# Expert pairs on column halves: w1/w3 products of both experts together, norm factor in the SiLU step, a fourth w2 buffer, and an output tail in pieces

## What is computed

```python
def hier_moe(h, w_grp, b_grp, w_exp, b_exp, w1, w3, w2):
    t = h.reshape(-1, D)                       # h = rms_norm(x, norm2_g)
    pg = softmax(t @ w_grp + b_grp)            # 4 groups, top 1
    el = (t @ w_exp + b_exp)[chosen group]     # 8 experts of it, top 2
    ...
    hid = silu(einsum('td,edf->tef', t, w1)) * einsum('td,edf->tef', t, w3)
    hid = hid * combine[..., None]
    out = einsum('tef,efd->td', hid, w2)
# x = x + hier_moe(rms_norm(x, norm2_g), ...), then the final norm
```

## Time and profile before

| what | us |
|---|---|
| median of 3 runs | 1255.3 (1254.24 to 1257.63) |
| the profiled execution | 1259.09 |
| its span (first to last instruction) | 1257.4 |
| TensorE busy in the span | 1195.2 |
| VectorE busy | 707.4 |
| ScalarE busy | 408.1 |
| GpSimd busy | 37.8 |

### The profile page before, as it was taken

The page is one execution under the profiler, slowest core; times in us unless marked ns, Lnnn a source line. Parts: engine busy times, 40 slices in busy tenths (PEclk is TensorE's granted clock), DMA queues, the critical chain, the costliest instruction groups (busy, mean ns, idle before and its releaser), DMA issues.

```text
span 1257.4 us, 19349 instructions
## 1 busy us (share of the span) xinstructions
PE 1195.2 (95%) x7286; PEld 898.5 (71%) x7286; DVE 707.4 (56%) x1006; ACT 408.1 (32%) x462; POOL 37.8 (3%) x53
## 2 busy tenths in 40 slices
PE   7999999999999999999999998999999999999994
PEld 6888888888888888888888888555555444444441
DVE  5777555554666767667875546344554444444445
ACT  4444333334344354443344542111112111111113
POOL 1000000001002022000000000000000000000000
PEclk8999999999999999999999999999999999999998
DMA  8566565655655455555765683999999999999993
GB/s 273 169 192 208 168 193 174 190 177 167 197 164 166 142 167 167 167 167 190 247 178 164 231 306 127 363 405 425 425 425 425 426 425 425 425 424 425 425 424 147
DMA packets 170150, 336.57 MB, mean 268 GB/s; under 512 B 12144, under 2 KB 136192, under 8 KB 153088
## 3 DMA queue, kind: packets, MB, share of 16 engines
q1 hardware_dynamic: 165536, 335.69, 72.5%
q10 hardware_dynamic: 4576, 0.37, 0.3%
HBM read 333.93 MB, written 2.11 MB: 267 GB/s over the span
## 4 chain that ended last, share of the span: by engine, by line
PE 57%; issue 40%; DVE 1%; DMA 1%; ACT 0%; ACTq 0%; POOL 0%; POOLq 0%; DVEq 0%
PE ps L830 19%; PE ps L859 11%; PE ps L832 10%; PE ps L861 5%; PE ps L991 5%; PE ps L992 2%; PE ps L819 1%; DMA param_rows<-in_norm_g_dram 1%; PE ps L960 0%; PE ps L1011 0%; DVE wsplit L1176 0%; PE ps L846 0%; PE ps L848 0%; ACT wsplit L582 0%; PE ps L847 0%
## 5 line engine op out<-in xcount | busy, mean ns | idle before, releaser
L1176 DVE TENSOR_TENSOR wsplit<-wraw,wsplit 128x2048 fp32r<-128x2048 f32 x120 | 277.1, 2309 | 183.2 <-ACT wsplit L582 182.3
L830 PE MATMUL ps<-act_split,wsplit 128*128 128x512 f32 x1024 | 362.0, 398 | 0.0
L582 ACT ACTIVATE wsplit<-wraw 128x2048 fp32r<-128x2048 f32 x120 | 230.0, 1917 | 387.4 <-PE ps L832 203.1
L832 PE MATMUL ps<-act_split,wsplit 128*128 128x256 f32 x1024 | 286.6, 280 | 0.0
L830 PEld LDWEIGHTS ps<-act_split,wsplit 128*128 128x128 f32 x1024 | 192.2, 188 | 47.7 <-issue 1.8
L859 PE MATMUL ps<-wsplit,act_split 128*128 128x512 f32 x608 | 218.3, 403 | 2.1 <-DVE wsplit L1176 2.1
L832 PEld LDWEIGHTS ps<-act_split,wsplit 128*128 128x128 f32 x1024 | 193.2, 189 | 0.2
L861 PE MATMUL ps<-wsplit,act_split 128*128 128x256 f32 x608 | 171.4, 282 | 0.0
L859 PEld LDWEIGHTS ps<-wsplit,act_split 128*128 128x128 f32 x608 | 115.7, 190 | 30.7 <-issue 2.7
L1082 PE MATMUL ps<-w_a,xe 128*64 128x256 f32 x1024 | 115.4, 381 | 14.3 <-DMA w_a<-in_w_dram 12.1
L1647 DVE TENSOR_TENSOR hid<-sg,ps 128x128 f32<-128x128 f32 x32 | 9.2, 287 | 205.8 <-ACT sg L775 205.8
(11 more groups left out here) (287 smaller groups left out, 1149.8 us busy)
## 6 DMA issues: line engine op xcount, KB each, us to landing
w_a<-in_w_dram SPq DMA_DIRECT2D x96, 1024.0 KB, 18.3
w_b<-in_w_dram SPq DMA_DIRECT2D x96, 1024.0 KB, 22.0
wraw<-in_w_in_dram SPq DMA_DIRECT2D x88, 1024.0 KB, 5.1
wraw<-in_w_out_dram SPq DMA_DIRECT2D x16, 1024.0 KB, 5.1
wraw<-in_w_branch_m_dram SPq DMA_DIRECT2D x8, 1024.0 KB, 5.1
wraw<-in_w_branch_a_dram SPq DMA_DIRECT2D x8, 1024.0 KB, 5.1
xin<-in_x_dram SPq DMA_DIRECT2D x2, 1024.0 KB, 6.3
x<-in_x_dram SPq DMA_DIRECT2D x1, 2048.0 KB, 9.4
```

What stands on the lines that cost most here:

```text
L582: act.activation(wsplit[:, q % 2, :, 0], wraw[:, q % RAW], ACT.Copy).then_inc(rounded, 1)
L830: pe.matmul(banks[b], w[:, k, 0, b * P:(b + 1) * P], a, start=first and k == 0, stop=False)
L832: last = pe.matmul(banks[b][:, 0:T], w[:, k, 1, b * P:(b + 1) * P], a[:, 0], start=False, stop=last_half and k == HALF_K - 1)
L1176: dve.tensor_tensor(wsplit[:, q % 2, :, 1], wraw[:, q % RAW], wsplit[:, q % 2, :, 0].bitcast(F32), ALU.subtract).then_inc(split, 1)
```

## The change

1. **Hidden products by pairs.** `hidden` now takes both experts of a pair at once: for each chunk one matmul of 512 columns (w1 and w3 whole) for the first expert on column half 0 and one for the second on column half 1. There are 32 matmuls a pair, which were 64 of 256 columns. One sigmoid, two products, two transposes and one copy follow for both experts together. `xe` is two buffers.
2. **Norm factor.** `xe` is a plain copy of `xg`; the 17th gather group goes. Two small matmuls make a row `rms_row` of all tokens' factors instead, and VectorE's new step in `slots` picks the factor of each slot by it (`slot_rms`). The sigmoid takes it as its scale and the two products take it and `slot_both` (factor times slot weight) as scalars, so that w2's result needs no scaling. `slots` now runs ahead of the sigmoid.
3. **Loads.** w1/w3 buffers are in quarters: DMAs of 0.5 MiB with runs of 4 KB, twice as many. Each quarter of both experts is loaded again when `h_quarters` says that it is done. w2 of expert 0 moves to its own place (`x2hi` goes to where `x2` was, ScalarE's copy to `x2` falls away, and `make_x2` adds x2hi and x2lo to `x2` in two VectorE steps of 128x2048 in front of the first `slots`), and is loaded in front of w1/w3 of expert 1. w2 waits for each half of `rows`.
4. **First pair.** Its `xe_first` has a place of its own: the first expert's is copied by ScalarE, 12 chunks between the last evacuations (L782) and 4 behind the table load; the second's by VectorE.
5. **Scatter.** Groups 0, 1 behind the first quarter, 2, 3 behind the second, 4 to 7 behind the last.
6. **Tail.** `rows` of the last pair is cut after block 2, two groups of scatter lie between; rounding and subtraction of its right half are in two pieces; groups use four banks. The multiply by final_g moves from VectorE to GpSimd, in front of the root.

```diff
-        w2s = [[sb("w2_a0", [P, FC, D], at=AT_GATES + 32 * KB), sb("w2_b0", [P, FC, D], at=AT_WRAW + 32 * KB)],
+        w2s = [[sb("w2_a0", [P, FC, D], at=AT_QK + 16 * KB), sb("w2_b0", [P, FC, D], at=AT_WRAW + 32 * KB)],
...
-            for kh in range(2):
-                load_hidden(0, 0, kh)
+            for kq in range(QUARTERS):
+                load_hidden(0, 0, kq)
+            for h in range(2):
+                load_rows(0, 0, 0, h)
...
-            sp.wait_ge(xg_summed, DC + 1)
-            load_rows(0, lambda b: b, (0,))
...
-                    for b in range(2):
-                        sp.wait_ge(upper_used, i * (2 * chunks) + (2 * chunks - 1 + b))
-                        load_hidden(b, ds(i * 2 + (b + 2), 1), 0)
-                        sp.wait_ge(h_summed, i * (2 * chunks) + (2 * chunks + b))
-                        load_hidden(b, ds(i * 2 + (b + 2), 1), 1)
+                    for kq in range(QUARTERS):
+                        sp.wait_ge(h_quarters, (i - 1) * (QUARTERS * chunks) + (QUARTERS * (chunks - 1) + kq + 2))
+                        for b in range(2):
+                            load_hidden(b, ds(i * 2 + b, 1), kq)
...
+            pool.wait_ge(fing_loaded, 16)
+            for g, (t, n) in enumerate(tail_groups):
+                pool.wait_ge(x2_final, g + 1)
+                cols = slice(n * 512, (n + 1) * 512)
+                pool.tensor_tensor(x2g[:, t, cols], x2[:, t, cols], fin_g[:, cols], ALU.mult).then_inc(x2g_ready, 1)
             root(42, TT, M_HEADS + 3)
...
+            def silu_and_turn(s):
+
+                act.wait_ge(h_quarters, s * QUARTERS + (QUARTERS + 1))
+                act.wait_ge(slots_ready, s + 2)
+                act.wait_ge(hid_ready, s + 1)
+                act.activation(sg[:], ps[:, 0, 0:FC * P], ACT.Sigmoid, scale=slot_rms[:, 0:1]).then_inc(sg_ready, 1)
+                act.wait_ge(hid_turned, s + 2)
+                act.wait_ge(y_summed, s * 4 + 1)
+                act.activation(hidT[:].rearrange("p f n -> p (f n)"), ps[:, 1, 0:FC * P], ACT.Copy).then_inc(hidT_ready, 1)
...
+                for kq in range(QUARTERS):
+                    pe.wait_ge(w13_loaded[kq], i * 64 + 64)
+                    for k in range(QUARTER_K):
+                        for b in range(2):
+                            last = pe.matmul(ps[b * SLOTS:(b + 1) * SLOTS, 0].rearrange("p (w f) -> p w f", w=2),
+                                             operands[b][:, kq * QUARTER_K + k], w13[b][:, kq, :, k],
+                                             start=kq == 0 and k == 0, stop=kq == QUARTERS - 1 and k == QUARTER_K - 1)
+                    last.then_inc(h_quarters, 1)
...
+            def silu(s):
+
+                dve.wait_ge(sg_ready, s + 1)
+                dve.wait_ge(hid_turned, s + 1)
+                dve.wait_ge(slots_ready, s + 2)
+                steps_x.done(dve.scalar_tensor_tensor(hid[:], ps[:, 0, 0:FC * P], slot_rms[:, 0:1], sg[:], ALU.mult, ALU.mult))
+                dve.scalar_tensor_tensor(hid[:], ps[:, 0, FC * P:2 * FC * P], slot_both[:, 0:1], hid[:],
+                                         ALU.mult, ALU.mult).then_inc(hid_ready, 1)
```

More of the change, by code:

```diff
@@ L1060, in _ @@
             parts = [part[:].rearrange("p t (q c) -> p t c q", c=DC) for part in (x2hi, x2lo)]
[L1061 to L1063 removed]
+            for c in range(DC):
+                if c >= 8:
+                    pe.wait_ge((xg_act, xg_dve)[c % 2], (c - 8) // 2 + 1)
                 for t in range(TT):
[L1065 to L1067 removed]
@@ L1102, in rows, with turn_mix @@
-            def rows(load_no, s, slot):
-                pe.wait_ge(hidT_ready, s * 2 + 3)
+            pe.wait_ge(xg_dve, 5)
+            for t in range(TT):
+                last = pe.matmul(ps[:, 1, t * P:(t + 1) * P], ones[:], rms_diag[:, t], start=True, stop=True)
+            last.then_inc(rms_summed, 1)
+            def turn_mix(s):
+                pe.wait_ge(mix_ready, s + 1)
+                pe.wait_ge(slots_ready, s + 1)
+                pe.wait_ge(hidT_ready, s + 1)
+                for t in range(TT):
+                    last = pe.transpose(ps[:, 1, (FC + t) * P:(FC + t + 1) * P], mix[:, t], ident[:])
+                last.then_inc(mix_turned, 1)
@@ L1105, in rows, with turn @@
+            def turn(s):
+                pe.wait_ge(hid_ready, s + 2)
+                pe.wait_ge(hidT_ready, s + 1)
+                pe.wait_ge(slots_ready, s + 2)
+                for f in range(FC):
+                    last = pe.transpose(ps[:, 1, f * P:(f + 1) * P], hid[:, f * P:(f + 1) * P], ident[:])
+                last.then_inc(hid_turned, 1)
+            def rows(load_no, s, slot, ns=range(4)):
+                pe.wait_ge(hidT_ready, s + 2)
                 pe.wait_ge(ys_ready, s * 2 + 1)
-                for n in range(4):
+                for n in ns:
@@ L1148, in experts @@
+                turn(0)
                 rows(0, 0, 0)
[L1150 to L1162 removed]
@@ L1163, in experts, with hidden_and_scatter @@
-                pair(EXPERTS // 2 - 1, EXPERTS // 4 - 1, 1)
-                scatter(EXPERTS // 2 - 1, range(GROUPS_OUT))
+                def hidden_and_scatter(i, half):
+                    hidden(i, i, xe, [[lambda: scatter(i - 1, half, (0, 1))], [lambda: scatter(i - 1, half, (2, 3))],
+                                      [], [lambda: scatter(i - 1, half, (4, 5, 6, 7))]])
+                    turn(i)
+                with pe.Fori(0, N_PAIRS // 2 - 1) as j:
+                    hidden_and_scatter(j * 2 + 1, 0)
+                    rows(j, j * 2 + 1, 1)
+                    hidden_and_scatter(j * 2 + 2, 1)
+                    rows(j + 1, j * 2 + 2, 0)
@@ new lines, in pair @@
+                def pair(i, half):
+                    ys_split(i - 1)
+                    slots(i, half, (i - 1) * GROUPS_OUT + 1)
+                    add(i - 1, (0, 1, 2, 3))
+                    silu(i)
+                    add(i - 1, (4, 5, 6, 7))
+                with steps_x.loop(0, N_PAIRS // 2 - 1, 4) as j:
+                    for n in (1, 2):
+                        i = j * 2 + n
+                        pair(i, n % 2)
+                        copy_tokens(starts_of(i + 1, 0), i + 1)
+                        make_mix(i + 1, 0, i + 1)
```

387 lines of the change are left out of this document (191 added, 196 removed).

## The result

The changed kernel takes **1260.17 us** (median of 19 runs, 1255.44 to 1263.33), the kernel before 1255.42 beside it (1253.92 to 1260.02): ratio 1.0028, interval 1.0019 to 1.0037. That is 3.5 us slower, 2.4 to 4.6 by the interval. The forecast was 1253.0 with a range to 1258.5: the time lies outside it. The profiled run of after is one of its short ones: 1257.89 us, span 1256.2.

What follows compares the result with a forecast made beforehand. The prediction took the stream of expert weights to bound the expert stage. Its terms, -7.5 (start) + 5.7 (rate) + 0.3 (pair) - 0.95 (tail), gave -2.4 us and a forecast of 1253 us, range 1246.5 to 1258.5.

Steps and rivals of the forecast that it cites:

- What bounds the kernel: Expert stage: set by the stream of expert weights at 425 GB/s, 29.6 us a pair; TensorE waits in nearly every pair.
- All 16 pairs run behind the stream: Expert stage: every pair is paced by the weight stream, 29.59 us a pair, read from two issues six pairs apart.
- Part 1: Start of the weight stream: w2 of expert 0 loaded early and experts starting sooner move it from 794.9 to 787.4, gain 7.5 us.
- No pause: Start of the weight stream: after the change, places come free early enough that the stream doesn't stop again.
- Part 2: Rate of the weight stream: w1/w3 transfers cut in two, with 4 KB runs, cost 0.047 us a MiB over 120 MiB, +5.7 us.
- Part 3: Inside a pair: TensorE 27.9 us before, 27.7 after, hidden behind the stream except in the last pair, +0.3 us.
- still covered by 2.3 us: Inside a pair: TensorE's 27.7 us stay 2.3 us under the stream's 30.0, so only the last pair counts.
- Part 4: Tail, from the last w2 product to the end of the root: 19.25 us instead of 20.2, -0.95 us.
- R: Start of the last w2 product, from which the tail's times are counted; 1229.12 in the kernel before.
- the pause stays: Rival, start of the stream: it isn't continuous and the pause of 3.0 us stays, +0.6, 1256 us; 6%.
- TensorE becomes the bound: Rival, expert stage: needs 2.3 us more a pair, hidden steps of 0.50 instead of 0.43; +42 at 0.59; 3%.

Runs made afterwards that it cites:

- e5: e1 with SyncE requesting the w2 of pairs 3 to 10 before their w1/w3 instead of behind: 1257.06 us, ratio 0.9992 to the kernel before.
- e6: e1 with the prefetch undone, w2 of expert 0 requested after the gather again: 1257.68 us, ratio 1.0007 to the kernel before.
- e1: The changed kernel with filler matmuls where TensorE idles between the w1/w3 and w2 products: 1258.62 us, ratio 1.0013 to the kernel before.
- e3: The kernel before with each w1/w3 transfer cut in two along K (0.5 MiB, 4 KB runs), nothing else: 1262.76 us, ratio 1.0038.
- e12: The changed kernel with only the 4 filler matmuls behind scatter group 5: 1261.87 us, ratio 1.0042 to the kernel before.

## Why the prediction was wrong, step by step

- **What bounds the kernel: half right.** "All 16 pairs run behind the stream" rested on issues at 1007.85 and 1185.36, both in the second half. In the timeline of before, pairs 1 to 7 take 27.40 us without a wait for weights, and only from pair 8 on 29.6; the 15 waits of the earlier trace rows are about two in each of the late pairs, not one in nearly every pair. The places are full when the experts begin, and TensorE lives on that. Two issues in the first half would have shown it:

```profile
838.87 4.25 SPq L448 DMA_DIRECT2D w_a<-in_w_dram  x4
...
866.27 4.24 SPq L448 DMA_DIRECT2D w_a<-in_w_dram  x4
```

- **Part 1, the start: this is the step that failed.** The earlier start of TensorE was right (-1.76 for -1.85). The other 5.65 of the 7.5 us weren't there. The working took the stream of before as started at 794.9, though its own rows put the first data at 787.07 + 2.3 = 789.4; the 5.5 us between are pauses, and I let the change remove them all by "No pause". The claim counted when places come free, but not in which order SyncE asks for them: after hidden quarters 0 to 3, w2 stands in the queue. The pause moved from 810 to 835 (173 GB/s); e5 removes it by the order alone. No gain of the w2 prefetch itself is seen (e6). The stream of the first 100 us behind the first expert matmul says where the gain went. Before has 395 GB/s, so it lacks 7.1 us of a stream of 425, and 5.0 more in which the late w2 flowed; e5 has 391, 6.9 us short of 420:

```profile
783.35:883.35 100.00, 94.59 (x674) 52.70 (x676) 40.94 (x75) 15.94 (x30) 0.00 (x0) 1.00 0.97 395
780.60:880.60 100.00, 98.65 (x466) 40.23 (x466) 41.80 (x80) 9.20 (x13) 0.00 (x0) 1.00 0.97 391
```

So 12.1 us before became 11.2 in after (373), 9.5 without the fall in pair 0 (e1, 380) and 6.9 with the other order too; the forecast had 787.4 - 781.5 = 5.9. The order of requests cost 2.6 of it and the fall 1.7.
- **Part 2, the rate: right in kind.** 420 instead of 427, nothing on top for the doubled number. Of 5.7 us, e3 measured 4.0 in the third row and 4.8 by the ratio.
- **Part 3, inside a pair: wrong size, mostly covered.** Hidden steps of 0.43 were right, but the gap of the pairs in the loop is 4.63 us and the granted clock falls behind it. A pair takes 28.2 or 29.9 us and not 27.7, so "still covered by 2.3 us" became 1.8 or 0.1. TensorE's 27.9 us a pair before were also too many: it works 27.40, so the new form costs 0.8 us a pair instead of saving 0.2. In the last pair the gap was 4.23 for a forecast of 4.35. e1's third row is 0.4 us over e3's, whose rate is the same: that is everything else in the change together (pair, quarters, order, place of w2), and within the scatter. The fall in pair 0 costs some 1.1 to 1.7 more (after against e1; e12 against e1).
- **Part 4, the tail: right.** Multiplies of 1.24 us for a taken 1.2, root end at R + 19.27 for R + 19.25. The Trainium skill's (GPSIMD Engine Reference, Performance versus the Vector engine) estimate of 1.12 us, quoted with the forecast, is near but low: here 7.42/6 = 1.24. That the end fits to 0.02 is luck: the six multiplies begin at R + 11.20 for 11.3, take 7.42 for 7.2, the root 0.69 for 0.75, and the errors cancel.

Sum for the profiled run, from the runs: -1.76 (start) + 4.0 (rate, e3) + 0.4 (all else, e1 against e3) + 1.1 (clock, after against e1) - 1.0 (tail) = +2.7; the profiles differ by +2.75. The sum must close, since its middle terms are steps from one profile to the next; it shows their sizes, not that none is missing. The rival "the pause stays" had the mechanism but counted 3.0 of the 5.6 us; "TensorE becomes the bound" got 3% for a price of the steps, while it came, as far as it did, through the gap and the clock. In the expert stage of after neither engine is far ahead: 28.2 or 29.9 us a pair on TensorE beside 29.96 on the stream.

## What to carry to other kernels

Before crediting a prefetch, ask what the queue would otherwise carry at that time: if the next request can't be issued earlier, the bytes fill an idle stretch, and loading them earlier can gain little or nothing. A lost stretch of a stream is a pause with a cause (here the program order of the issuing engine); it goes only if the change removes that cause. Check the bound in the first and in the last third of a loop separately; where two engines are within 6% of each other, an edit to either shows only part of its price.
